# TensorE's program for the 32 experts: a loop over seven slots, or a straight line

## The reference, cut to what matters

```python
g_sel = jnp.argmax(g_logits, axis=-1)
top_p, top_i = lax.top_k(jax.nn.softmax(e_logits, axis=-1), MOE_TOPK)     # MOE_TOPK = 2
expert = g_sel[:, None] * MOE_PER_GROUP + top_i
...
gate = jnp.einsum('td,edf->tef', t, lp['w_exp_gate'])                     # 32 experts, 1024 x 256
up = jnp.einsum('td,edf->tef', t, lp['w_exp_up'])                         # 32 experts, 1024 x 256
act = jax.nn.silu(gate) * up * w_tok[..., None].astype(t.dtype)
out = jnp.einsum('tef,efd->td', act, lp['w_exp_down'])                    # 32 experts, 256 x 1024
```

## Time and profile before

| | us |
|---|---|
| median of three runs | 803.72 |
| the profiled execution | 803.58 |
| its span, first to last instruction | 801.5 |
| TensorE busy with products in the span | 730.4 (91%) |
| VectorE, ScalarE, GpSimd busy | 276.4, 182.5, 99.9 |
| the first gate product of the experts | at 562.71 |
| the last expert's first gate product | at 774.15 |

### The profile page before, as it was taken

How to read it: one execution, slowest core, us unless ns; L and a number is a source line. 1 busy time by engine, 2 the same in 40 slices (tenths; PEclk the granted TensorE clock), 3 DMA queues, 4 the chain that set the end, 5 groups by cost and what they waited for, 6 DMA issues and landing times.

```text
span 801.5 us, 20045 instructions
## 1 busy us (share of the span) xinstructions
PE 730.4 (91%) x8430; PEld 528.5 (66%) x8431; DVE 276.4 (34%) x766; ACT 182.5 (23%) x461; POOL 99.9 (12%) x238
## 2 busy tenths in 40 slices
PE   5799999999989998898987999996899989989986
PEld 3567777887766666776766777873565656656644
DVE  0216613440134443675675122124222222222224
ACT  1311123122731323113122301123111111111115
POOL 7000000000011034000000100001222222222200
PEclk9999999999999999999999899999899999999999
DMA  9953779899335866740001704939899999999951
GB/s 305 292 170 130 253 256 319 306 324 334 107 100 132 236 162 154 243 152 27 2 2 58 297 1 195 417 155 343 334 409 413 412 413 410 416 411 413 412 204 60
DMA packets 108729, 195.89 MB, mean 244 GB/s; under 512 B 9964, under 2 KB 71097, under 8 KB 100488
## 3 DMA queue, kind: packets, MB, share of 16 engines
q1 hardware_dynamic: 106760, 189.94, 65.7%
q0 software_dynamic: 1920, 5.25, 1.8%
HBM read 185.40 MB, written 9.77 MB: 244 GB/s over the span
## 4 chain that ended last, share of the span: by engine, by line
PE 77%; DMA 9%; DVE 6%; issue 4%; ACT 3%; SPq 1%; ACTq 0%; DVEq 0%; POOLq 0%
PE ps L1265 17%; PE ps L625 8%; PE ps L1337 7%; PE ps L605 5%; PE ps L638 4%; PE ps L463 4%; PE ps L491 4%; DMA arena<-in_w_exp_down 3%; PE ps L1182 3%; DMA arena<-in_w_ada 3%; PE ps L608 2%; DMA arena<-in_w_in 2%; PE ps L467 2%; PE ps L595 2%; DVE arena L2025 1%
## 5 line engine op out<-in xcount | busy, mean ns | idle before, releaser
L1265 PE MATMUL ps<-arena 128*128 128x288 f32 x576 | 143.9, 408 | 1.3 <-DMA arena<-in_w_in 0.9
L1265 PEld LDWEIGHTS ps<-arena 128*128 128x128 f32 x576 | 108.3, 190 | 33.4 <-DVEq L1932 2.0
L625 PE MATMUL ps<-arena 128*32 128x128 f32 x2432 | 77.3, 281 | 15.6 <-issue 12.1
L625 PEld LDWEIGHTS ps<-arena 128*32 128x32 f32 x2432 | 67.5, 113 | 31.9 <-issue 30.8
L1337 PE MATMUL ps<-arena 128*128 128x288 f32 x256 | 76.9, 430 | 5.1 <-ACT arena L1764 3.0
L1337 PEld LDWEIGHTS ps<-arena 128*128 128x128 f32 x256 | 45.7, 195 | 21.5 <-issue 9.6
L605 PE MATMUL ps<-level,arena 32*128 32x256 f32 x624 | 45.8, 408 | 0.5 <-DVE arena L874 0.5
L638 PE MATMUL ps<-arena,hact 128*32 128x256 f32 x608 | 40.7, 385 | 0.0
L437 POOL DMA_INDIRECT arena<-h_rows,idx_now x38 | 37.6, 989 | 9.4 <-issue 9.4
L868 DVE TENSOR_TENSOR h_row<-h_row,ps 128x64 f32<-128x64 f32 x38 | 8.4, 221 | 85.1 <-ACT h_row L726 85.1
L1182 PE MATMUL ps<-arena,cT 128*32 128x128 f32 x1024 | 33.5, 289 | 3.8 <-DMA arena<-in_w_ada 3.7
(11 more groups left out here) (474 smaller groups left out, 997.0 us busy)
## 6 DMA issues: line engine op xcount, KB each, us to landing
arena<-in_w_exp_gate SPq DMA_DIRECT2D x32, 1024.0 KB, 23.6
arena<-in_w_exp_up SPq DMA_DIRECT2D x32, 1024.0 KB, 24.2
arena<-in_w_exp_down SPq DMA_DIRECT2D x32, 1024.0 KB, 23.8
arena<-in_w_ada SPq DMA_DIRECT2D x12, 2048.0 KB, 10.1
arena<-in_w_in SPq DMA_DIRECT2D x18, 1024.0 KB, 5.4
arena<-in_w_ada_final SPq DMA_DIRECT2D x4, 2048.0 KB, 14.9
arena<-in_w_in SPq DMA_DIRECT2D x16, 512.0 KB, 5.5
arena<-in_state_ssm_rec SPq DMA_DIRECT2D x8, 512.0 KB, 6.5
```

The costliest lines, as they stand in the source:

```text
L625: l = mm(ps[CW * q:CW * (q + 1), 5, 0:P].rearrange("p (g f) -> p g f", g=2), xwin[:, at:at + CW], gate_up[:, :, k, f:f + HF], start=(k == ...
L1265: l = mm(ps[:, 2 + 2 * sl + m, 0:TOK], w_ring[sl][:, k, m * P:(m + 1) * P], HN[:, k, :], start=(k == 0), stop=(k == KT - 1))
```

## The change

The loop of four rounds is gone, and so is the straight part for the last four experts. All 32 experts are written out one after the other, so `windows` stands 32 times in TensorE's program in place of eleven. Addresses in `tab` and the values waited for are constants, and `first` is read once. The loop over one expert's windows stays.

```diff
             e.wait_ge(S("tab"), 1)
-            with e.Fori(0, E // ESLOT) as i:
-                first = e.value_load(tab[0:1, 0, bass.ds(i * ESLOT, 1)], min_val=0, max_val=MAXWIN)
-                for s in range(ESLOT):
-                    e.wait_ge(S(f"ex_ld{s}"), i * 48 + (48 + (32 if s < 4 else 0)))
-                    end = e.value_load(tab[0:1, 1, bass.ds(i * ESLOT + s, 1)], min_val=1, max_val=MAXWIN)
-                    windows(first, end, s)
-                    first = end
-            rest = E % ESLOT
-            first = e.value_load(tab[0:1, 0, E - rest:E - rest + 1], min_val=0, max_val=MAXWIN)
-            for s in range(rest):
-                e.wait_ge(S(f"ex_ld{s}"), E // ESLOT * 48 + 48 + 32)
-                end = e.value_load(tab[0:1, 1, E - rest + s:E - rest + s + 1], min_val=1, max_val=MAXWIN)
+            first = e.value_load(tab[0:1, 0, 0:1], min_val=0, max_val=MAXWIN)
+            for x in range(E):
+                t, s = divmod(x, ESLOT)
+                e.wait_ge(S(f"ex_ld{s}"), t * 48 + 48 + (32 if s < 4 else 0))
+                end = e.value_load(tab[0:1, 1, x:x + 1], min_val=1, max_val=MAXWIN)
                 windows(first, end, s)
                 first = end
             combined(end, last=True)
```

## The result

The changed kernel takes 806.04 us against 804.24 us before (medians of 20 runs each, 800.87 to 810.00 and 796.14 to 806.94); the ratio of the runs is 1.0039, 95% interval 1.0021 to 1.0057, so 1.7 to 4.6 us slower (this ratio and those below are formed from the single runs and can differ from the quotient of the medians, here 1.0022). The forecast, 804.3 and no change, named too small a loss. The profiled execution took 808.25 us, its span 806.1; that is 4.7 us over the profiled one before, more than the runs' 1.7 to 4.6, so the sizes read from this trace are those of a slower than usual execution.

A forecast was written before the change was run, and what follows sets the result against it. TensorE paces the stage early, the weight stream its end. Entry -0.5 and instruction fetch +1.2 move the last landing +0.7 us, from 803.58 to 804.3; range 802.5 to 807.1, the first case alone 802.5 to 805.7.

The forecast's parts named there:

- TensorE's saving, about 7.7 us, hidden by the weight stream: Back edges, exit and ordinary expert steps get quicker by about 7.7 us, which come back as waits for weights.
- 10 or more: Profile sign: TensorE's wait on w_exp_down grows from 3.4 to 10 us or more, spread over experts 27 to 31.
- The rival in which it is the end's time: Expert stage: the weight stream has hidden slack, so all 8.1 us of TensorE's saving come through, 795.5; chance 0.10.
- Entry, 0.5 us: Before the first gate product: constant table addresses start it, and so the weight stream, 0.5 us earlier; bounds 0 and 1.1.
- Instruction fetch: Expert stage: code of 21 further bodies is fetched through the busy DMA engines, adding 1.2 us; bounds 0 and 2.1.
- 18 more packets: Count of added instruction packets, 0.84 per body, at 0.065 us of the whole stream each: 1.2 us.
- The upper bound of the term, 2.1 us: Instruction fetch at most: 0.115 us per packet, from the weight queue's rate with packets, 382.3 against 389.2 GB/s.
- a slow last window: Rival at expert 31: its products run at a lowered clock, costing 1.4 us, 805.7 in all; chance 0.35.
- All packets on one engine: Rival in the weight stream: 18 packets delay one DMA engine 18.7 us, 821.8; chance 0.07, shared with late code.
- The clock at the last window: Rival: waits before experts 27 to 31 lower TensorE's clock, expert 31 loses 1.4 us, 805.7; chance 0.35.
- slow and fast windows alternate: Experts 27 to 31: a slow window lasts 1.4 us longer and shortens the next wait, which should leave the clock up.
- its row of 600 to 700 us: Profile row before the change: two back edges with a single instruction packet, read as back edges costing 1.38 us without a fetch.

The follow-up runs named there:

- c1: Kernel before, with gate, up and down weight reloads from expert 7 on cut to a sliver: 796.32 us, ratio 0.9926.
- c2: Changed kernel with gate, up and down weight reloads from expert 7 on cut to a sliver: 787.7 us, ratio 0.9816 to the kernel before.
- b1: Kernel before plus 19 transfers of 16 KB from ScalarE, each in 16 pieces of 1 KB over all 16 DMA engines: 804.33 against 802.44 us, ratio 1.0023.
- a4: Kernel before plus 19 transfers from ScalarE's queue, each 17 pieces of 960 B on one DMA engine: 812.05 us, ratio 1.0097.
- c3: Kernel before, SyncE's reloads written out, 12 one-engine 16 KB transfers behind reloads of experts 7 to 18: 808.72 against 804.02 us, ratio 1.0079.
- c4: Kernel before, SyncE's reloads written out, 12 one-engine 16 KB transfers behind reloads of experts 20 to 31: 808.57 against 804.02 us, ratio 1.0071.
- a1: Changed kernel again without an edit: 807.06 against 803.72 us for the kernel before, ratio 1.005.
- a2: Changed kernel with two extra table reads before experts 7, 14, 21 and 28: 805.78 us, ratio 1.0036 to the kernel before.
- a3: Kernel before with the four single experts ahead of the loop and expert 0's table reads before the first transposes: 803.73 against 803.72 us, ratio 0.9998.
- b3: Changed kernel with experts 0 to 17 straight, then two loop rounds for experts 18 to 31: 807.1 us, ratio 1.006 to the kernel before.

## Why the prediction was wrong, point by point

*TensorE's saving, about 7.7 us, hidden by the weight stream: right.* Issue time fell by 10.3 us, the waits before experts 27 to 31 add up to 1.06 + 2.48 + 1.93 + 3.24 + 1.01 = 9.7 us, just short of the "10 or more" that was forecast, and without the stream the saving comes through as 8.6 us (c1, c2). The rival in which it is the end's time is wrong for this kernel and right for c2.

*Entry, 0.5 us: right in the profile,* 2.38 to 1.88 us, though too small to be seen in the times.

*Instruction fetch, "18 more packets", each "0.065 us of the whole stream": the step that failed.* The packets came as counted (27 - 9 = 18) and their mean load too (1.25 us for 1.2). The failure is the division by 16: the term was sized by the mean of all engines, and the landing came 4.7 us later where +0.7 was forecast. The division holds for work dealt over all engines, as b1's 1 KB pieces; an instruction packet holds a single engine for some 1.1 us (0.9% of 209 us on 16 engines over 27 packets), 1.4 with the delay of the data packet behind it. The stream's end is that of its slowest engine (a4 against b1), and a lag is not made good later (c3 as c4). In the straight line eight engines were late (shares of 0.48 to 0.52 from 772 to 775). If those eight carry the packets evenly, that is 18 x 1.4 / 8 = 3.2 us in place of 1.2, an estimate: with the entry's 0.5 off it is +2.7 us or 806.3, in the middle of the measured +1.7 to +4.6 (the profiled execution's stage lost 4.1). Which engine takes which packet the trace doesn't tell, so that the share of eight stays argued. The upper bound of the term, 2.1 us, was made from the weight queue's mean rate, and so had the same fault. That 806.04 lies within the stated 802.5 to 807.1 is luck: the part of that range above 805.7 was there for a slow last window, and the profile after shows a fast one.

*All packets on one engine: wrong in its extreme, right in its mechanism.* It got a small chance because nine packets before left no long end. That excluded one engine, not several; the same row falls from 447 to 268 GB/s and then on in steps, which might have been read as engines that finish apart. The cases between 1 engine and 16 were missing, and the result lies in one of them.

*The clock at the last window: not the cause.* It came at full clock in the profile after (1.96 us) and in a1 (1.95), and the loss was there. It came slow in a2 (3.53), and in kernels with a loop as well: 3.08 us in a3, 3.54 in b1. That slow and fast windows alternate behind the waits was right for the profile after: experts 27 to 31 took 1.95, 2.71, 1.95, 2.92 and 1.96 us. The 1.4 us of a slow last window can fall to either kernel; how often it fell to each in the runs without a profile is not known.

## What to carry to other kernels

Where the DMA engines are full, count code as traffic, and count it on the engine that carries it: a load that is not dealt over all of them delays the end by the lag of its fullest engine, however small its mean share (a4: 0.4% in the mean, 7.8 us at the end). Unrolling pays where the engine that runs the code sets the time (c2, 8.6 us), and costs where a saturated stream does (+0.39%). Before trusting a mean share, read how the stream ends: here a fall within some 2 us went with an even load (b1), and a step at half height with eight late engines.

## What the runs showed of the hardware that was not expected

A lag of a DMA engine in a full stream is kept: 12 transfers of 16 KB in the first half cost 0.79%, in the second 0.71% (c3, c4).

An instruction packet takes a whole engine out of a full stream: 15.2 weight packets under way in place of 16.2 for about 1.1 us, and 0.27 to 0.55 us more for the data packet behind it.

A back edge may or may not fetch. The loop over seven, at the start of the stage, went back three times without a packet to speak of the earlier trace rows; the same seven bodies behind a straight line of 18 cost 8.52 + 2.08 us at their back edge, with three packets within 20 us, and five from 741 to 771 us (b3). The Trainium skill, Runtime: NRT & Kernel Launch, section Instruction fetch mechanics, says that a taken branch whose target isn't loaded has to wait for it; b3's trace agrees, with the 8.52 us. The same section of the Trainium skill also calls crossing into the next block mostly hidden; for TensorE's own program that holds here too (1.8 us of issue time before all gate products of the stage), and the price appears in the weights instead. The prediction held its row of 600 to 700 us against this rule; that row shows only that the loop stayed loaded there. Why it did so in one place and not in the other is open.
